# Turns of dilated queries and keys between products, their copies on ScalarE, vector 13 in the attention, output slices one ahead

## The reference, cut to what matters

```
def adaln_norm(x, c, g, w_ada, b_ada):
    mod = silu(c) @ w_ada + b_ada
    shift, scale, gate = split(mod, 3)
    return rms_norm(x, g) * (1.0 + scale) + shift, gate

def dilated_mixer(h, w_in, w_out):          # 16 heads of 64
    q, k, v, z = split(h @ w_in, 4, axis=-1)
    q, k = rope(q), rope(k)
    ...  # causal softmax attention in three groups of heads: window 128,
    ...  # every 4th key, every 16th key; a group is weighed by its mean exp(lse)
    return (o * silu(z)) @ w_out
```

## Time and profile before

| | |
|---|---|
| device time, three runs | 1197.33, 1192.49, 1197.65 us (median 1197.33) |
| profiled execution, own time | 1192.64 us |
| its span | 1190.8 us |
| mean granted TensorE clock | 0.989 |
| busy: PE / PE weight load / DVE / ACT / POOL | 93% / 78% / 72% / 46% / 13% |
| moved by DMA | 221.56 MB, mean 186 GB/s |

### The profile page before, as it was taken

How to read it: one execution, slowest core, us unless ns; L and a number is a source line. 1 busy time by engine, 2 the same in 40 slices (tenths; PEclk the granted TensorE clock), 3 DMA queues, 4 the chain that set the end, 5 groups by cost and what they waited for, 6 DMA issues and landing times. The chain is left out here.

```text
span 1190.8 us, 19663 instructions
## 1 busy us (share of the span) xinstructions
PE 1107.9 (93%) x7522; PEld 929.6 (78%) x7522; DVE 856.0 (72%) x1435; ACT 549.2 (46%) x989; POOL 149.1 (13%) x108
## 2 busy tenths in 40 slices
PE   5898899998998999999999999898988999999997
PEld 5686688786786778878778867888978877888886
DVE  5867788799785899965599746757495566865654
ACT  1353674532664534444477654442141335454442
POOL 0010231121412000001000001005051020000020
PEclk9999999998999999999999999998899999999999
DMA  8875346489653699965465543931011245956561
GB/s 318 295 266 197 123 126 230 139 269 301 194 163 118 216 338 344 333 221 179 134 203 165 189 142 96 328 124 56 20 37 39 98 130 172 342 177 195 175 185 65
DMA packets 143389, 221.56 MB, mean 186 GB/s; under 512 B 10850, under 2 KB 66615, under 8 KB 143169
## 3 DMA queue, kind: packets, MB, share of 16 engines
q1 hardware_dynamic: 140532, 216.39, 55.3%
q10 hardware_dynamic: 2765, 3.93, 0.9%
HBM read 219.24 MB, written 1.05 MB: 185 GB/s over the span
## 5 line engine op out<-in xcount | busy, mean ns | idle before, releaser
L566 ACT CAST w_parts<-ring 128x1024 fp32r<-128x1024 f32 (+2 forms) x288 | 290.1, 1037 | 259.7 <-DMA ring<-in_w_ffn_up 71.6
L571 DVE TENSOR_TENSOR w_parts<-ring,w_parts 128x1024 fp32r<-128x1024 f32 (+2 forms) x276 | 338.7, 1265 | 82.9 <-ACT w_parts L566 76.5
L612 PE MATMUL bank<-w_parts,lhs_hi 128*128 128x512 f32 (+2 forms) x960 | 382.1, 398 | 11.0 <-issue 5.5
L614 PE MATMUL bank<-w_parts,lhs_lo 128*128 128x512 f32 (+2 forms) x960 | 373.6, 389 | 0.0
L627 PE MATMUL bank<-w_parts,lhs_hi 128*128 128x512 f32 (+2 forms) x960 | 260.5, 390 | 6.4 <-DVE w_parts L571 6.3
L612 PEld LDWEIGHTS bank<-w_parts,lhs_hi 128*128 128x128 f32 x960 | 182.0, 190 | 48.9 <-issue 8.7
L627 PEld LDWEIGHTS bank<-w_parts,lhs_hi 128*128 128x128 f32 x960 | 178.6, 189 | 44.2 <-DVE w_parts L571 11.2
L614 PEld LDWEIGHTS bank<-w_parts,lhs_lo 128*128 128x128 f32 x960 | 182.1, 190 | 32.1 <-issue 1.0
L760 DVE SCALAR_TENSOR_TENSOR ada_acc<-ring,c_act,ada_acc 128x512 f32<-128x512 f32 x203 | 165.7, 816 | 14.6 <-DMA ring<-in_ada_w 3.2
L612 PE MATMUL bank<-w_parts,up_hi 128*128 128x512 f32 x176 | 68.7, 390 | 0.0
L614 PE MATMUL bank<-w_parts,up_lo 128*128 128x512 f32 x176 | 68.5, 389 | 0.0
(11 more groups left out here) (360 smaller groups left out, 1375.5 us busy)
## 6 DMA issues: line engine op xcount, KB each, us to landing
ring<-in_w_ffn_up SPq DMA_DIRECT2D x176, 256.0 KB, 4.1
ring<-in_w_ada SPq DMA_DIRECT2D x72, 512.0 KB, 5.0
ring<-in_ada_w SPq DMA_DIRECT2D x48, 512.0 KB, 4.8
ring<-in_w_ffn_down SPq DMA_DIRECT2D x44, 512.0 KB, 4.5
ring<-in_w_in SPq DMA_DIRECT2D x44, 512.0 KB, 4.5
ring<-in_dil_w_in SPq DMA_DIRECT2D x32, 512.0 KB, 4.7
ring<-in_nsa_w_in SPq DMA_DIRECT2D x20, 512.0 KB, 4.6
ring<-in_w_in SPq DMA_DIRECT2D x20, 416.0 KB, 4.2
```

Source lines behind the costliest of these rows:

```text
L566: eng.copy(hi, raw).then_inc(hi_ready, 1)
L571: eng.tensor_tensor(lo, raw, hi.bitcast(F32), ALU.subtract).then_inc(lo_ready[who], 1)
L612: pe.matmul(b, x_hi, w, start=(k0 + k == 0), stop=False)
L614: mm = pe.matmul(b, x_lo, w, start=False, stop=False)
```

## The change

It has four parts. (1) The turns of q and k are put between the matmuls of outputs 4 and 5: q turns 0 and 1 after matmuls 24 and 36 of output 4; q turns 2 and 3 after matmuls 8 and 16 of output 5; k turns 0 and 1 after 28 and 40; k turn 2, the sum of half 11 and k turn 3 behind it. (2) ScalarE copies all eight of them; `turns("dil_q", 4, "act")` and the same for k. The readers of later turns are unchanged. (3) Half 13 is no longer accumulated before the attention but within it: `vector_steps` does one step at even and two at odd calls, 24 instead of 16 in all, and the units stand in the list accordingly. (4) `stream_ahead("dve", "dil_out", 0)` has its default of one output's lead of two units instead of none, so two rests of `("dil_out", 1)` stand before the collecting of halves 12 to 15.

```
-    behind = ((), (10, 10), (10, 10), (11, 11), (11, 11, 12, 12), (12, 12, 13, 13, 13, 13))
+    behind = ((), (10, 10), (10, 10), (11, 11), (11, 11, 12, 12), (12, 12))
...
-    s.append(beside([(("dil", 6 + j), dw, 512 * (6 + j)) for j in range(2)], range(14, 16), 1))
+    big = [(("dil", 6 + j), unit) for j in range(2) for unit in column_units([(dw, 512 * (6 + j), 512)], 512, KC)]
+    small = iter([(("ada", n), unit) for n in (13, 14, 15) for unit in ada(n)[2]])
+    order = []
+    for i, unit in enumerate(big):
+        order += [unit] + [next(small) for _ in range(1 + i % 2)]
+    s.append(("beside", [key for key, _ in order], [unit for _, unit in order], act))
...
 def dil_dve(dve, link):
+            stream_to("dve", plan.outputs["dil", 4][1][3])
             stream_ahead("dve", "dil", 4)
             ada_collect_up_to(11)
-            read_turns("dve", "dil_q", lambda b: dil_qT[:, 2 * b:2 * b + 2, :].rearrange("p c t -> p (c t)"), range(4))
-            stream_to("dve", plan.outputs["ada", 13][1][-1])
-            read_turns("dve", "dil_k", lambda b: dil_kT[:, 2 * b:2 * b + 2, :].rearrange("p c t -> p (c t)"), range(4))
+            stream_to("dve", plan.outputs["dil", 5][1][3])
+            stream_to("dve", plan.outputs["ada", 12][1][-1])
             ada_collect_up_to(12)
...
+            def vector_steps(i):
+                for step in range(3 * i // 2, 3 * (i + 1) // 2):
+                    ada_beside(13 + step // 8, step % 8)
...
-            dil_att.dve(dve, link, weigh, lambda i: ada_beside(14 + i // 8, i % 8), shift_tops, first_half)
+            dil_att.dve(dve, link, weigh, vector_steps, shift_tops, first_half)
...
-            stream_ahead("dve", "dil_out", 0, 0)
+            stream_ahead("dve", "dil_out", 0)
             ada_collect_up_to(16)
...
 def dil_act(act):
+            stream_to("act", plan.outputs["dil", 4][1][3])
+            turned_rows("dil_q", dil_qT, 0)
+            turned_rows("dil_q", dil_qT, 1)
             for j in (4, 5):
...
                 if j == 4:
-                    read_turns("act", "dil_q", lambda b: dil_qT[:, 2 * b:2 * b + 2, :].rearrange("p c t -> p (c t)"), range(4))
+                    turned_rows("dil_q", dil_qT, 2)
+                    turned_rows("dil_q", dil_qT, 3)
+                    stream_to("act", plan.outputs["dil", 5][1][3])
+                    turned_rows("dil_k", dil_kT, 0)
+                    turned_rows("dil_k", dil_kT, 1)
                 if j == 5:
-                    read_turns("act", "dil_k", lambda b: dil_kT[:, 2 * b:2 * b + 2, :].rearrange("p c t -> p (c t)"), range(4))
+                    turned_rows("dil_k", dil_kT, 2)
+                    turned_rows("dil_k", dil_kT, 3)
...
 def dil_pe(pe):
+            ada_sum(pe, 10)
+            steps = gemm_steps(pe, "dil", 4, from_lhs, "norm1", 512)
+            pe.wait_ge(rope_done, 12)
+            for b in range(2):
+                for _ in range(24 - 12 * b):
+                    next(steps)
+                turn_tokens(pe, "dil_q", dil_rows(dil_q), [b])
+            for _ in steps:
+                pass
+            steps = gemm_steps(pe, "dil", 5, from_lhs, "norm1", 512)
+            for name, b, n in (("dil_q", 2, 8), ("dil_q", 3, 8), ("dil_k", 0, 12), ("dil_k", 1, 12)):
+                for _ in range(n):
+                    next(steps)
+                if (name, b) == ("dil_k", 0):
+                    pe.wait_ge(rope_done, 16)
+                turn_tokens(pe, name, dil_rows(dil_q if name == "dil_q" else dil_k), [b])
+            for _ in steps:
+                pass
+            turn_tokens(pe, "dil_k", dil_rows(dil_k), [2])
+            ada_sum(pe, 11)
+            turn_tokens(pe, "dil_k", dil_rows(dil_k), [3])
```

More of the change, by code:

```diff
@@ L1898, in dil_dve, with turned_rows @@
             turned_left_dve(dve, "dil_o", range(2, 4))
-            stream_ahead("dve", "dil_out", 0, 0)
+            stream_ahead("dve", "dil_out", 0)
             ada_collect_up_to(16)
         def dil_act(act):
+            def turned_rows(name, d, b):
+                read_turns("act", name, lambda b: d[:, 2 * b:2 * b + 2, :].rearrange("p c t -> p (c t)"), [b])
+            stream_to("act", plan.outputs["dil", 4][1][3])
+            turned_rows("dil_q", dil_qT, 0)
+            turned_rows("dil_q", dil_qT, 1)
             for j in (4, 5):
@@ L1925, in dil_pe, with dil_rows @@
         def dil_pe(pe):
-            for j in range(6):
-                if j:
-                    gemm(pe, "dil", j, from_lhs, "norm1", 512)
-                if j in (3, 5):
-                    ada_sum(pe, 10 if j == 3 else 11)
-                if j == 4:
-                    pe.wait_ge(rope_done, 12)
-                    turn_tokens(pe, "dil_q", lambda tt, c: dil_q[:, tt, 2 * c:2 * c + 2, :].rearrange("p h d -> p (h d)"), range(4))
-                if j == 5:
-                    pe.wait_ge(rope_done, 16)
-                    turn_tokens(pe, "dil_k", lambda tt, c: dil_k[:, tt, 2 * c:2 * c + 2, :].rearrange("p h d -> p (h d)"), range(4))
+            def dil_rows(d):
+                return lambda tt, c: d[:, tt, 2 * c:2 * c + 2, :].rearrange("p h d -> p (h d)")
+            for j in range(1, 4):
+                gemm(pe, "dil", j, from_lhs, "norm1", 512)
+            ada_sum(pe, 10)
[12 more added lines that the diff above has]
+                if (name, b) == ("dil_k", 0):
+                    pe.wait_ge(rope_done, 16)
+                turn_tokens(pe, name, dil_rows(dil_q if name == "dil_q" else dil_k), [b])
[4 more added lines that the diff above has]
+            turn_tokens(pe, "dil_k", dil_rows(dil_k), [3])
             await_turns_read(pe, "dil_k", range(4))
@@ L3029, in turn_order @@
     t += turns("kw", 1, "act") + turns("qp", 4) + turns("qr", 4) + turns("pc", 1, "act")
-    t += turns("nsa_o", 4, "dve") + turns("norm1", 4, "dve") + turns("dil_q", 4) + turns("dil_k", 4)
+    t += turns("nsa_o", 4, "dve") + turns("norm1", 4, "dve") + turns("dil_q", 4, "act") + turns("dil_k", 4, "act")
     t += turns("dil_o", 4, "dve")
```

## The result

The changed kernel took 1183.37 us (median of five runs, 1180.84 to 1187.08), the kernel before 1197.59 us in the five runs beside them (1192.49 to 1198.24). The recorded ratio is 0.9913 with a 95% interval from 0.9890 to 0.9935: faster by 0.9%. It is not the quotient of these two medians, which is 0.988. The forecast was 1186.5 us with a range of 1180.5 to 1194.5. Beside the later experiments the kernel before ran 67 more times, with medians of 1192.62 to 1192.97 us in three groups. So its usual level is that of its profiled execution, 1192.64 us, and not the 1197 us of the first runs; against it the changed kernel's median is 0.992.

A forecast was written before the change was run, and what follows sets the result against it. PE bounds the kernel, so only its waits and slow clock count. Terms -7.8 + 0.5 - 2.3 = -9.6 us give 1183.0 from the profile, 1187.7 from the median; forecast 1186.5, range 1180.5 to 1194.5.

The forecast's parts named there:

- Turns of q and k, -7.8: Output 4 to first scores: PE's waits for copies and slow clock go, scores start at 294.4 to 294.6 instead of 302.35.
- Half 13 in the attention, +0.5: Attention: eight more VectorE steps, 6.3 us, mostly hidden in 9.3 us of free time; costs 0.5 us, ends 0 and 6.3.
- I count 1 us of it as likely, still under the cover: Attention: of at most 10.9 us more that GpSimd rests could hold VectorE, 1 us is likely, against 3.0 us left.
- the cover of 3.0 us: Attention: VectorE's free time left, 9.3 us before, once half 13's eight steps (6.3 us) are added.
- Rival B: Attention: VectorE falls behind, shut out by GpSimd's rests; sum -5.7 us, 1187 or 1191.6 us; chance 0.10.
- The lead of slices, -2.3: Around the collecting: two rests move into VectorE's idle time, gated half and norm chain come 2.3 us earlier, between 0 and -3.1.
- The sum of -9.6: Whole change: -7.8 for the turns, +0.5 for half 13 in the attention, -2.3 for the lead of slices.
- A: Before the attention: ScalarE is late, its copies behind casts waiting for transfers; 1186.9 or 1191.6 us; chance 0.15.
- D: Turns: each of eight waits for its predecessor's copy behind a waiting cast, PE's clock falls; slower, 1211 or 1215.6; chance 0.07.
- C: Behind the attention: the lead brings nothing because the next output's casts come late; -7.3, 1185.3 or 1190.0 us; chance 0.06.

The follow-up runs named there:

- The crossed kernels: Kernel before with only half 13 moved into the attention: ratio 1.0014; changed kernel with half 13 put back ahead of the attention: ratio 0.9963.
- the kernel with short rests: Changed kernel with GpSimd's rests of outputs 6 and 7 formed over 64 of 1024 columns only, the remainder left out: attention 41.43 us.

## Why the prediction was right, and where it was not

**Turns of q and k, -7.8.** Measured -7.95, and by the steps named: one wait for a rest (0.98 us, 1.0 foretold), the clock at 1.00, no wait for a copy, ScalarE last before the scores. But I booked it to the turns. The crossed kernels show that it belongs to turns and half 13 together: with the old list and order of half 13 S1 + S2 did not shrink at all in the traced execution, and by some 2 us by whole times. The text had the link (the slot of output 6's second unit is now freed by a rest of output 5), but not its price, 7.2 us by the traces, and not that the gate on VectorE would have been as late.

**Half 13 in the attention, +0.5.** The term was mis-sized: +1.28, and +0.30 in S3, where PE waits 0.4 us for the gating. The step that failed is "I count 1 us of it as likely, still under the cover". (The row behind it was read a little wrong: the step of the earlier trace rows ends at 330.80 us, 0.55 us behind its rest, and not with it.) Taking 0.71 us for an undisturbed step (17.05 / 24), the 16 steps of before (16.1 us in all, their first steps included) lost 4.7 us to GpSimd and the 24 lose 6.9, so 2.2 us were added, not 1. And the cover of 3.0 us was counted over the whole attention, while PE needs each mask at its time. VectorE still stood idle for 3.6 of the 42.75 us when PE waited for it: two steps stretched one after the other, at 322.84 and 326.05, made the last masks late. Rival B was the right mechanism: it had 3.9 us more than the forecast, and 1.1 came.

**The lead of slices, -2.3.** Measured -2.25, alone and in the change. PE's waits for rests there shrank from 3.1 to 1.1 us, where 0.8 was foretold.

**The time.** The sum of -9.6 gave 1183.0 from the profile's own time; the median was 1183.37. An agreement within 0.4 us is luck: the stretches gave -8.6, 1.0 less than the sum, and the five runs lie between 1180.84 and 1187.08. The forecast of 1186.5 was 3.1 us too high because I leaned to the median of three runs, which the later runs of the same kernel did not bear out.

**Rivals.** A and D did not occur in the change, but A's mechanism did where half 13 stayed ahead of the attention. C is refuted by S4. What remains open is how the 7.2 us divide between ring slots and VectorE's order, whether the change has a part in the shorter time behind S4, and why the kernel before ran at 1197 us in four of its first five runs.

## What to carry to other kernels

Two edits that look separate can be one: test whether a freed engine finds its next operand in the ring before booking the gain to the edit that freed it. Count cover per deadline, not per stage: 3 us of idle time in 41 us did not hide a 2.2 us delay. Whenever a cast or any other producer is moved earlier, check which GpSimd instruction it starts and which VectorE instruction that falls on, since where an exclusion falls can matter more than a step more or less (26.8 us for 24 steps, 23.9 for the same 24). And stretches cut at the same matmul tell 0.1 us apart where whole times tell 3, as long as the clock did not fall in one of them: then a second execution, or the whole times, must bear it out.

## What the runs showed of the hardware

The hold-up also strikes an instruction with a single tensor from SBUF: the first step of a half (L759) took 2.46 us beside a rest, and 0.48 us in the kernel with short rests. The Trainium skill, SBUF — State Buffer, "Who interferes with whom", counts the scalar form among those that can contend, in its two-port modes; the trace agrees as to the hold-up, and no row shows which mode it ran in. A copy out of PSUM within a rest was not held up, 0.56 us where others take 0.55:

```profile
313.05 2.65 POOL L576 TENSOR_TENSOR w_parts<-ring,w_parts 128x1024 fp32r<-128x1024 f32 x1 [4.14 <-ACT w_parts L571]
314.47 0.56 DVE L721 COPY arena<-bank 128x384 f32<-128x384 f32 x1 [1.02 <-PE bank L1247]
```

PE's clock fell behind a single gap of 2.08 us in a busy attention (granted 0.55 over the next 7.3 us), and stayed at 1.00 behind gaps of 1.68, 1.70 and 1.18 us. The length of the gap alone does not decide it: in the changed kernel the clock was at 0.50 from 385.9 to 389.3 us, behind the 1.67 us of idle time that end at 385.17, and at 1.00 behind a gap of 2.37 us at 758.47.
